# First mixture of a two-block forward pass: layer two in four column chunks, its rows added back by row groups, and semaphores for further passes

## What is computed

```python
logits = xt @ w_router + b_router
top_v, top_e = lax.top_k(logits, 4)             # of 32 experts
weights = softmax(top_v)
def expert_block(tok, e):                       # the rows that chose expert e
    hcat = x_pad[tok] @ w1[e] + b1[e]           # 1024 -> 2048
    x_glu = jnp.minimum(hcat[:, ::2], 7.0)
    x_lin = jnp.clip(hcat[:, 1::2], -7.0, 7.0)
    act = x_glu * jax.nn.sigmoid(1.702 * x_glu) * (x_lin + 1.0)
    return act @ w2[e] + b2[e]                  # 1024 -> 1024
out = jnp.sum(y[dest].reshape(T, 4, D) * weights[..., None], axis=1)
```

## Time and profile before

| | us |
|---|---|
| median of 3 runs | 2355.33 |
| lowest and highest | 2343.31, 2359.2 |
| the profiled execution | 2362.85 |
| its span in the trace | 2361.0 |
| first bias matmul of the first mixture (from the span's start) | 440.8 |
| its last layer two ends | 1474.9 |

### The profile page before, as it was taken

One profiled execution on the slowest core, in us unless ns is written; L12 is line 12 of the kernel. 1 busy time (PEld: TensorE's weight loads), 2 busy tenths in 40 slices (PEclk: granted clock), 3 DMA queues, 4 the chain that ended last, 5 costly groups with the idle time before them and its releaser, 6 DMA issues. The chain is left out here.

```text
span 2361.0 us, 28284 instructions
## 1 busy us (share of the span) xinstructions
PE 1889.7 (80%) x11518; PEld 852.9 (36%) x11518; DVE 811.2 (34%) x1618; ACT 496.6 (21%) x1005; POOL 76.8 (3%) x96
## 2 busy tenths in 40 slices
PE   6999998888988988789987888669887755555565
PEld 4655545433333333323333333345434422222221
DVE  2224332333333244433444335595493300000001
ACT  2022201123232133332333233222201100000000
POOL 0000000000000000000000000390000000000000
PEclk9999998899999989989999899789988787877877
DMA  8745257497797699998999999333115389999996
GB/s 288 255 145 184 82 188 302 182 384 329 299 400 303 275 424 393 423 424 357 404 423 423 424 402 419 111 107 107 39 54 195 161 355 427 428 428 427 428 423 270
DMA packets 113956, 713.56 MB, mean 302 GB/s; under 512 B 16703, under 2 KB 21006, under 8 KB 68654
## 3 DMA queue, kind: packets, MB, share of 16 engines
q1 hardware_dynamic: 105344, 704.98, 73.5%
q10 hardware_dynamic: 8398, 5.47, 0.8%
HBM read 709.35 MB, written 1.07 MB: 301 GB/s over the span
## 5 line engine op out<-in xcount | busy, mean ns | idle before, releaser
L780 PE MATMUL ps<-ring,ar 128*32 128x512 f32 x3072 | 388.4, 643 | 48.3 <-DMA ring<-in_w 25.6
L434 PE MATMUL ps<-ar 128*128 128x128 f32 (+5 forms) x1750 | 358.1, 362 | 37.6 <-PEq L692 11.4
L441 PE MATMUL ps<-ring,ar 128*32 128x512 f32 x1536 | 209.2, 706 | 193.3 <-DMA ring<-in_w_gate 81.4
L434 PEld LDWEIGHTS ps<-ar 128*128 128x128 f32 (+2 forms) x1750 | 236.3, 201 | 159.9 <-issue 102.0
L434 PE MATMUL ps<-ring,ar 128*128 128x512 f32 (+2 forms) x624 | 261.5, 579 | 8.7 <-DVE ar L1245 3.2
L780 PEld LDWEIGHTS ps<-ring,ar 128*32 128x32 f32 x3072 | 99.7, 116 | 334.0 <-issue 285.8
L1604 DVE TENSOR_SCALAR ar<-ps 128x256 f32<-128x256 f32 x128 | 54.4, 425 | 448.8 <-PE ps L780 442.1
L791 PE MATMUL ps<-ring,ar 128*32 128x512 f32 x1536 | 175.3, 595 | 22.1 <-ACT ar L2187 21.7
L538 PE MATMUL ps<-ring,ar 128*128 128x512 f32 x384 | 172.8, 598 | 15.6 <-ACT ring L2250 15.6
L441 PEld LDWEIGHTS ps<-ring,ar 128*32 128x32 f32 x1536 | 60.5, 127 | 335.9 <-issue 335.0
L434 PEld LDWEIGHTS ps<-ring,ar 128*128 128x128 f32 x624 | 118.5, 192 | 146.0 <-issue 134.4
(11 more groups left out here) (387 smaller groups left out, 1312.1 us busy)
## 6 DMA issues: line engine op xcount, KB each, us to landing
ring<-in_w SPq DMA_DIRECT2D x192, 2048.0 KB, 18.1
ring<-in_w_gate SPq DMA_DIRECT2D x32, 2048.0 KB, 17.7
ring<-in_w_up SPq DMA_DIRECT2D x32, 2048.0 KB, 16.7
ring<-in_w_down SPq DMA_DIRECT2D x32, 2048.0 KB, 16.1
ring<-in_w_in SPq DMA_DIRECT2D x21, 2048.0 KB, 8.1
ring<-in_w_ada SPq DMA_DIRECT2D x12, 2048.0 KB, 8.8
ring<-in_w_out SPq DMA_DIRECT2D x4, 2048.0 KB, 8.0
ring<-in_w_branch SPq DMA_DIRECT2D x6, 1024.0 KB, 5.0
```

Of the source, the lines that this page charges most:

```text
L434: ins = self.t.e.matmul(o, l, r, start=(i == 0), stop=(i == len(pairs) - 1))
L441: ins = self.t.e.matmul(b[32 * i:32 * i + 32, :], l, r, start=(k == 0), stop=(k == len(steps) - 1))
L780: ins = e.matmul(b[32 * s:32 * s + 32, :], HG[:, 2 * c + r, 32 * n:32 * n + 32], W[:, r, HALF(s)], start=False, stop=(c == 3 and r == 1))
```

## The change

1. `layer2`: four groups of 32 array columns, each with another 256 of the 1024 outputs, and the whole contraction summed in place: 32 matmuls of 256 columns a pass in place of 16 of 512. A pass's result is 128 partitions (chunk, row) by 256, and `evict` is one copy of it.
2. `spread1`: for each pass and each half of the tokens four matmuls with 32 partitions (one chunk each) and 256 columns, into banks 4 to 7. Only the passes that the expert has are added (passes 2 and 3 together). It stands between the two halves of layer one of the next expert. VectorE adds four times 128x512 whatever the number of rows, ahead of its work on layer one.
3. Further passes signal on semaphores of their own (`s_px` for pass 1, `s_py` for passes 2 and 3 of layer two, `s_ps` for the spread). `either` waits in its Else part for those alone, `only` has no Else part. Freeing a slot needs `s_pe`, `s_px` and `s_py`.
4. Turns ahead: turn 0 stands inside the next expert's gather, turn 1 ahead of layer two of pass 0, the turn of passes 2 and 3 ahead of layer two of pass 1. Their completion is signalled by the first matmul of the layer two behind them. The weight matrix has two transposed halves, the second only where the next expert has over 64 rows.
5. ScalarE's order is new; the selection, the activations and their turned copy have one buffer in place of two, VectorE's temporaries are at other places. The number of rows is loaded once an expert. The second mixture and the other parts of the kernel compute as before.

```diff
+                if held[i][0] in ("w1", "w2"):
+                    q.wait_ge(s_px, px[("free",) + held[i]])
+                    q.wait_ge(s_py, py[("free",) + held[i]])
...
-    def either(q, u, limit, body, count=None):
-        n, met = q.n, dict(q.met)
-        if count is None:
-            count = q.e.value_load(flag(u))
-        with q.e.If(count > limit):
+    def only(t, count, limit, body):
+        n, met = t.n, dict(t.met)
+        with t.e.If(count > limit):
             body()
-        q.met = met
-        with q.e.Else():
-            q.e.wait_ge(q.sem, n)
-            q.e.nop().then_inc(q.sem, q.n - n)
+        assert t.n == n
+        t.met = met
+    def either(t, x, count, limit, body):
+        n, m, met = t.n, x.n, dict(t.met)
+        with t.e.If(count > limit):
+            body()
+        assert t.n == n
+        t.met = met
+        with t.e.Else():
+            if m > 0:
+                t.e.wait_ge(x.sem, m)
+            t.e.nop().then_inc(x.sem, x.n - m)
...
+        x, y, z = Queue(e, s_px), Queue(e, s_py), Queue(e, s_ps)
...
+        def rows_in(u, h, lane):
+            t.wait_ge(s_act, act["rows", 1])
+            b = w.claim("hg", 1, u, h, lane=lane)
+            for k in range(4):
+                m = w.sums(b[:, TB(k)], [(XNV[:, tb, TB(4 * h + k)], SB1[:, tb, :]) for tb in range(2)])
+                pe["hg", 1, u, h, k] = m
+        def gather1(u, count, between):
+            pe["sw1", u, 0] = t(weights_turned(u, 0, (4,)))
+            rows_in(u, 0, (5,))
+            between()
+            only(t, count, 64, lambda: weights_turned(u, 2, (6,)))
+            rows_in(u, 1, (4,))
+            pe["sw1", u, 2] = pe["hg", 1, u, 1, 0]
+        def spread1(u, count):
+            b = [w.claim("sp", u, c, lane=(SP1[c],)) for c in range(4)]
+            def rows(n, tb, first, last):
+                for c in range(4):
+                    r = slice(32 * c, 32 * c + 32)
+                    ins = e.matmul(b[c][:, 256 * tb:256 * tb + 256], SWT1[u % 2][r, n, TB(tb)], YG1[r, n, :],
+                                   start=first, stop=last)
+                return ins
+            t.wait_ge(s_act, act["yg", u, 0])
+            n, met = z.n, dict(t.met)
+            with e.If(count > 32):
+                for tb in range(2):
+                    t.wait_ge(s_act, act["yg", u, 1])
+                    rows(1, tb, True, False)
+                    def later():
+                        t.wait_ge(s_act, act["yg", u, 3])
+                        rows(2, tb, False, False)
+                        rows(3, tb, False, False)
+                    only(t, count, 64, later)
+                    ins = rows(0, tb, False, True)
+                z(ins)
+            t.met = met
+            with e.Else():
+                for tb in range(2):
+                    ins = rows(0, tb, True, True)
+                ins.then_inc(s_ps, z.n - n)
+            psp["sp", u] = z.n
+        counts = [e.value_load(flag(0))]
+        gather1(0, counts[0], lambda: None)
...
-            def layer2(b, n, arrive):
+            def layer2(b, n, arrive, first):
                 for s in range(4):
                     if arrive and s % 2 == 0:
                         w.weights("w2", u, s // 2)
                     W = RG_(slot["w2", u, s // 2], 0, 2, 2, 1024)
-                    for h in range(2):
-                        for r in range(2):
-                            ins = e.matmul(b[64 * h + 32 * r:64 * h + 32 * r + 32, :],
-                                           AT_[:, 2 * s + r, 32 * n:32 * n + 32], W[:, s % 2, r, HALF(h)],
-                                           start=(s == 0), stop=(s == 3))
+                    for r in range(2):
+                        for c in range(4):
+                            ins = e.matmul(b[32 * c:32 * c + 32, 0:256], AT1[:, 2 * s + r, 32 * n:32 * n + 32],
+                                           W[:, s % 2, r, 256 * c:256 * c + 256], start=(s == 0 and r == 0),
+                                           stop=(s == 3 and r == 1))
+                            if first is not None:
+                                first(ins)
+                                first = None
                 return ins
...
+                        ins = e.transpose(b[:, TB(2 * i + r)], AC1[:, n, TB(r)], ident)
+                return ins
...
+            def turn_first():
+                pe["at", u, 0] = t(turn_act(0, (0,), (7,)))
+            b0 = w.claim("l1", u, 0, lane=(0,))
             for half in range(2):
-                done = t(layer1(bl[0], 0, half, True))
-                def further():
-                    if half == 0:
-                        bl.extend(w.claim("l1", u, n, lane=(n,)) for n in (1, 2, 3))
-                    with e.If(count > 64):
-                        with e.If(count > 96):
-                            layer1(bl[3], 3, half, False)
-                        layer1(bl[2], 2, half, False)
-                    t(layer1(bl[1], 1, half, False))
-                either(t, u, 32, further, count)
+                m = t(layer1(b0, 0, half, True))
+                pe["l1", u, half] = m
+                if half == 1 and u + 1 < NE:
+                    counts.append(e.value_load(flag(u + 1)))
+                def passes():
+                    def fourth():
+                        w.claim("l1", u, 3, lane=(3,)) if half == 0 else None
+                        layer1(ps("l1", u, 3), 3, half, False)
+                    def later():
+                        only(t, count, 96, fourth)
+                        w.claim("l1", u, 2, lane=(2,)) if half == 0 else None
+                        layer1(ps("l1", u, 2), 2, half, False)
+                    only(t, count, 64, later)
+                    w.claim("l1", u, 1, lane=(1,)) if half == 0 else None
+                    x(layer1(ps("l1", u, 1), 1, half, False))
+                either(t, x, count, 32, passes)
                 for c in (2 * half, 2 * half + 1):
                     w.free("w1", u, c)
-            pe["l1", u, 0], pe["l1x", u] = done, t.n
-            if u > 0:
-                spread(t, w, 1, u - 1, TL1)
-            turn_act(0, (0,))
+                    px["free", "w1", u, c], py["free", "w1", u, c] = x.n, 0
+                if half == 0 and u > 0:
+                    spread1(u - 1, counts[u - 1])
+            px["l1", u] = x.n
             if u + 1 < NE:
-                gather(t, w, 1, u + 1, TL1)
+                gather1(u + 1, counts[u + 1], turn_first)
+            else:
+                turn_first()
+            only(t, count, 32, lambda: turn_act(1, (1,), (5,)))
             t.wait_ge(s_act, act["at", u, 0])
-            pe["l2", u, 0] = t(layer2(w.claim("l2", u, 0, lane=(7,)), 0, True))
+            def first_second(ins):
+                pe["at", u, 1] = t(ins)
+            pe["l2", u, 0] = t(layer2(w.claim("l2", u, 0, lane=(7,)), 0, True, first_second))
             def second():
-                turn_act(1, (1,))
+                def first_third(ins):
+                    px["at", u, 2] = x(ins)
+                only(t, count, 64, lambda: turn_act(2, (2, 3), (6,)))
                 t.wait_ge(s_act, act["at", u, 1])
-                pe["l2", u, 1] = t(layer2(w.claim("l2", u, 1, lane=(1,)), 1, False))
+                x(layer2(w.claim("l2", u, 1, lane=(1,)), 1, False, first_third))
             def later():
-                turn_act(2, (2, 3))
-                b = [w.claim("l2", u, n, lane=(n,)) for n in (2, 3)]
                 t.wait_ge(s_act, act["at", u, 2])
-                with e.If(count > 96):
-                    layer2(b[1], 3, False)
-                pe["l2x", u] = t(layer2(b[0], 2, False))
-            count = e.value_load(flag(u))
-            either(t, u, 32, second, count)
-            either(t, u, 64, later, count)
+                def fourth():
+                    layer2(w.claim("l2", u, 3, lane=(3,)), 3, False, None)
+                only(t, count, 96, fourth)
+                y(layer2(w.claim("l2", u, 2, lane=(2,)), 2, False, None))
+            either(t, x, count, 32, second)
+            px["l2", u] = x.n
+            either(t, y, count, 64, later)
+            py["l2", u] = y.n
             for g in range(2):
                 w.free("w2", u, g)
-        spread(t, w, 1, NE - 1, TL1)
+                px["free", "w2", u, g], py["free", "w2", u, g] = x.n, y.n
+        spread1(NE - 1, counts[NE - 1])
...
+    def vector_select1(v, u):
+        if u > 0:
+            v.wait_ge(s_pe, pe["hg", 1, u - 1, 1, 3])
+        v(v.own.tensor_tensor(SB1, bc(iota, 1, [128, 2, 128]), RK[:, :, u:u + 1].to_broadcast([128, 2, 128]),
+                              ALU.is_equal))
+        for tb in range(2):
+            four = bc(SB1[:, tb].rearrange("p (n s) -> p n s", n=4), 2, [128, 4, 4, 32])
+            k = v(v.own.tensor_scalar(SWB1[:, tb].rearrange("p (n c s) -> p n c s", n=4, c=4), four,
+                                      CMB[:, tb, u:u + 1], None, ALU.mult))
+        dve["sel", 1, u] = k
...
```

(70 more changed lines are left out.)

213 lines of the change are left out of this document (114 added, 99 removed).

## The result

| | before | after |
|---|---|---|
| median of 4 runs each (us) | 2357.26 | 2395.61 |
| lowest and highest | 2343.31, 2361.45 | 2393.98, 2396.71 |
| the profiled execution, its span | 2362.85, 2361.0 | 2395.52, 2393.7 |
| first bias to the last layer-two record of the first mixture | 1033.5 | 1070.4 |

The ratio is 1.0173, its 95% interval 1.0129 to 1.0216: slower by 1.7%. The forecast was 2279. The profiled executions differ by 33 us, and the first mixture by 37: all of the loss lies there.

What follows compares the result with a forecast made beforehand. TensorE bounds experts 0 to 9, weight loads the rest. Layer two ending at 1406 instead of 1474.9 gains 69, the tail 7: in sum -76, median 2355.33 to 2279, range 2252 to 2320.

Steps and rivals of the forecast that it cites:

- The bound before: First mixture: TensorE bounds experts 0 to 9, loads later; expert 9 ends at 770 (816.0 before), layer two at 1406 (1474.9).
- Layer two in four chunks: Layer two on TensorE: 64 records of 256 columns take 3.6 us a pass as now, 56 ns each.
- The rival of 111 ns a record: Layer two bound by issue: a pass costs 3.5 us more, the median is 2374; chance 6%.
- Spread: Adding an expert's rows on TensorE: 1.0 us after one pass, 1.85 after two, 3.6 after three, where it was 3.9.
- Turns ahead: Transposes placed earlier: layer two starts 5 us behind layer one; a 0.8 us wait stays in three-pass experts.
- The step that failed: TensorE's drains replaced by two or three more branches, free while work is queued; put in at 1.0 us an expert.
- The rival of the chains: Products, ScalarE's copies and code fetches leave 4, 2 and 1.5 us in three-, two- and one-pass experts; median 2313; chance 20%.
- The rival of the clock: TensorE's granted clock falls to 0.87, experts 0 to 9 take 367 us; median 2329; chance 7%.
- The tail: Behind the first mixture's layer two, to the spread's last add: 5.0 us in place of 12.0, gain 7.

Runs made afterwards that it cites:

- e1: The kernel after with an expert limited to 96 rows and pass 3 taken out on TensorE, VectorE and ScalarE: 2303.42 us, ratio to before 0.9783.
- e10: e1 with 76 matmuls an expert that never run put back into TensorE's program alone: 2385.71 us, ratio to before 1.0114.
- e5b: The kernel after with weight pieces of the first mixture, from the eighth on, loading only 32 of 128 partitions: 2259.59 us, ratio to before 0.9588.
- e9: The kernel after with weight pieces of the first mixture, from the eighth on, loading only 8 of 128 partitions: 2192.09 us (one execution).

## Why the prediction was wrong

The forecast was 2279 and the time 2396, 117 us more.

- **The bound before.** Read rightly. In e1, where the program comes mostly in time, expert 9 ends at 766.3 us (forecast 770) and layer two at 1414.6 (forecast 1406). Its branches still take 184 us, so this is not the forecast's own case.
- **Layer two in four chunks.** Right: 64 records in 3.66 us, 57 ns each (forecast 3.6 and 56), and no wait beside them (1.2 us in all). The rival of 111 ns a record is out. The Trainium skill (TensorE: Matmul & The Clock Gate, section Back-to-back issue gap) gives 62 ns a matmul with hardware decode off; that does not bind here, since every record has a weight load beside it and the pair takes 57.
- **Spread.** 1.15 us for 16 records and 3.7 for 64 (forecast 1.0 and 3.6). The timelines show no gap at a change between column groups and row groups, but the starts do. Four records of layer one (512 columns) start together, and the next four start 410 ns after the last of them; the spread's first record starts 523 ns after it. From the spread's last record to layer one it is 304 ns, where it is 196 ns to the next four of the spread. So such a change costs about 0.11 us, which the forecast's sum did not have.
- **Turns ahead.** Right. Layer two starts 4.5 to 5.0 us behind layer one in experts of two and three passes (forecast 5), and 4.5 to 5.1 in all of e1 but the last; in after's one-pass experts a late block can make it up to 10.8. A three-pass expert has one wait of 0.8 us there, as said. Expert 8 (compare), after:

```profile
734.18 1.15 PE L810 MATMUL ps<-ar 32*128 32x256 f32 x16
735.26 10.51 PE L854 MATMUL ps<-ring,ar 128*32 128x512 f32 x96
...
750.73 3.66 PE L866 MATMUL ps<-ring,ar 128*32 128x256 f32 x64
755.19 0.63 PE L879 MATMUL ps<-ar 128*128 128x128 f32 x4 [0.80 <-DVE ar L1724]
755.74 7.11 PE L866 MATMUL ps<-ring,ar 128*32 128x256 f32 x128
```

  It runs from 717.9 to 762.8 us, 44.9 (forecast about 44, before 52.7). Heavy experts are as forecast: they execute their code, and have 44 us for its packets.
- **The step that failed.** "What replaces them is branches alone, two or three more than now. They cost nothing while TensorE has work queued [...] I put in 1.0 us an expert." I saw branches from 70 ns to 6.0 us and took the long ones for rare accidents of a branch. They are the fetch of the next block, and its price goes by the amount of code, not by the number of branches. The amount had been in front of me: layer two's matmuls double in all four passes, run or not, and with the spread's two versions the code grows by 41%. Against the 1.0 us an expert, TensorE's branches took 10.8 us an expert in after (346 us in all), where they had taken 4.4 before (140 us). The term should have been, per one-pass expert, packets times 5.7 to 6.1 us against 29.7. Measured, one-pass experts take 30.5 us on average in after (26.8 in e1, 26.9 before; the last expert left out), where the forecast had them under 20 when loads don't hold them. Here the code holds them, and the loads wait for the slots.
- **The rival of the chains** named code fetches but priced them as 1.5 us in one-pass experts. Right in kind, too small by far.
- **The clock** came as a consequence, not by itself: 0.89 in after, 0.93 in e1, and 0.89 again in e10 with the code alone put back, where it makes 32 us. It makes the most of the 41 us of busy time between after and e1. The rival of the clock expected 0.87 in experts 0 to 9; there it was 0.94, and 0.87 behind them.
- **The tail.** Before 12.0 us, forecast 5.0. In after the spread's matmuls start at 1517.93, 4.30 us late for a fetch, and the last add ends at 1522.4, 8.8 us behind layer two.
- **The sum of the miss.** Of the 117 us, 92 go with pass 3 (2396 to 2303): 83 are the code, by e10, and 9 the rest of its work. Of the other 24, 9 are in e1's mixture, 5 in its tail (10 us, again with a late spread), and 10 come from setting the median 8 us under the profiled execution, where e1's is 2 above it.

## What to carry to other kernels

Count the instructions of an engine's program per unit of time, also those in branches that never run, and see on the page's instruction queue how many blocks come in a stage: where blocks times their distance reaches the time of the stage's bound, a matmul split in two can cost more than its execution shows. Long compare-and-branch records, waits put down to a semaphore long reached, and "issue" gaps within a group of equal matmuls are the signature. When splitting doubles the code, look first for passes that never run, and take them out or share their code.

## What the runs showed of the hardware that had not been expected

- TensorE's program comes in packets of 16 KB, some 250 matmuls' and weight loads' instructions each, and the more the weights load, the slower it comes. In one-pass experts of the old kernel, with the loads at 415 GB/s, the packets are at least 5.6 us apart (median 6.3); in the new kernel's at 113 GB/s (e5b) at least 3.4, at 38 GB/s (e9) 3.05.
- A block that is jumped over is brought too: 104 matmuls that never run cost 166 us in 32 experts.
- The branches of over 2 us end 1.4 us (median) after a packet of the program has ended, in every run, with the loads at 38 to 405 GB/s.
- Halving the packets of w1 (8 KB) changes nothing in this: 2398 us against 2396.
- Code has a knee: 0.3 us a packet between 2.97 and 3.78 packets an expert (old kernel), 2.1 us from 4.06 to 5.28 and 3.1 from there to 6.34 (new kernel).
- A change between column groups and row groups adds about 0.11 us between the starts of records: 523 ns for 410 behind records of 512 columns, 304 for 196 behind records of 256.
